# Compressed attention for eight heads at once, with block-diagonal keys and values, in a two-block transformer kernel

## The reference

```python
dist = (t[:, None] - cmp_end[None, :]).astype(jnp.float32)
valid = dist >= 0
s = jnp.einsum('bghqd,bgnd->bghqn', q_c, k_cmp) * scale
s = jnp.where(valid, s - slopes * dist, NEG)
p_cmp = jax.nn.softmax(s, axis=-1) * valid.any(-1, keepdims=True)
o_cmp = jnp.einsum('bghqn,bgnd->bghqd', p_cmp, v_cmp)
...
o = g_c[0] * o_cmp + g_c[1] * o_slc + g_c[2] * o_win
```

## Time and profile before

| what | value |
|---|---|
| median of 3 runs | 1159.49 us (1159.38 to 1160.04) |
| the profiled execution, its own time | 1160.29 us |
| its span, first to last instruction | 1158.5 us |
| PE busy | 1083.8 us, 94% |
| DVE busy | 666.1 us, 57% |
| ACT busy | 510.3 us, 44% |
| POOL busy | 64.1 us, 6% |
| attention, from the MLP of the compressed keys to `b_out` | 355.5 to 467.5 us |

### The profile page before, as it was taken

One profiled execution on the slowest core, in us unless ns is written; L12 is line 12 of the kernel. 1 busy time (PEld: TensorE's weight loads), 2 busy tenths in 40 slices (PEclk: granted clock), 3 DMA queues, 4 the chain that ended last, 5 costly groups with the idle time before them and its releaser, 6 DMA issues.

```text
span 1158.5 us, 17658 instructions
## 1 busy us (share of the span) xinstructions
PE 1083.8 (94%) x7447; PEld 959.1 (83%) x7447; DVE 666.1 (57%) x1099; ACT 510.3 (44%) x780; POOL 64.1 (6%) x103
## 2 busy tenths in 40 slices
PE   6985999999999977999999998999998989999997
PEld 6863799999989854799999987899666978999996
DVE  4975456555556498555555567646444535555554
ACT  5322344343443377454443444435344544444442
POOL 3000084000010000000000000000000000000000
PEclk9997999999997998999999999999899999999999
DMA  8765247666656300647666644553224505565540
GB/s 230 197 194 133 75 144 219 184 180 186 200 106 205 111 1 1 204 144 216 187 179 188 202 136 145 184 182 110 73 73 145 169 14 182 185 215 175 189 146 37
DMA packets 192633, 175.14 MB, mean 151 GB/s; under 512 B 15878, under 2 KB 168326, under 8 KB 192554
## 3 DMA queue, kind: packets, MB, share of 16 engines
q1 hardware_dynamic: 190584, 170.69, 48.6%
q10 hardware_dynamic: 1874, 3.30, 0.8%
q0 software_dynamic: 96, 0.02, 0.0%
HBM read 172.06 MB, written 1.93 MB: 150 GB/s over the span
## 4 chain that ended last, share of the span: by engine, by line
PE 82%; DVE 11%; ACT 3%; DMA 2%; issue 1%; SPq 1%; POOLq 0%; POOL 0%; ACTq 0%; DVEq 0%
PE bank L1630 24%; PE bank L1631 24%; PE bank L1632 24%; DVE split_lo L995 2%; PE bank L1798 2%; ACT split_hi L622 1%; DVE soft L1273 1%; DVE soft L1292 1%; PE bank L1655 1%; DMA act<-u_rows 1%; PE bank L1645 1%; DVE v L1367 1%; DVE xn_lo L1012 1%; PE bank L1866 1%; PE bank L2057 1%
## 5 line engine op out<-in xcount | busy, mean ns | idle before, releaser
L995 DVE TENSOR_TENSOR split_lo<-raw,split_hi 128x2048 fp32r<-128x2048 f32 (+1 forms) x157 | 355.7, 2271 | 195.3 <-ACT split_hi L622 195.2
L1630 PE MATMUL bank<-xn_hi,split_hi 128*128 128x256 f32 x1440 | 413.2, 287 | 5.7 <-DVE split_lo L995 3.5
L1631 PE MATMUL bank<-xn_lo,split_hi 128*128 128x256 f32 x1440 | 409.5, 284 | 0.0
L1632 PE MATMUL bank<-xn_hi,split_lo 128*128 128x256 f32 x1440 | 409.3, 284 | 0.0
L622 ACT ACTIVATE split_hi<-raw 128x2048 fp32r<-128x2048 f32 (+1 forms) x157 | 296.0, 1889 | 153.9 <-PE bank L1632 146.1
L1630 PEld LDWEIGHTS bank<-xn_hi,split_hi 128*128 128x128 f32 x1440 | 278.1, 193 | 12.2 <-issue 4.4
L1631 PEld LDWEIGHTS bank<-xn_lo,split_hi 128*128 128x128 f32 x1440 | 278.2, 193 | 1.4
L1632 PEld LDWEIGHTS bank<-xn_hi,split_lo 128*128 128x128 f32 x1440 | 278.0, 193 | 0.0
L1630 PE MATMUL bank<-split_hi,ffa_hi 128*128 128x512 f32 x320 | 125.4, 392 | 1.8 <-DVE ffa_lo L995 1.8
L1631 PE MATMUL bank<-split_lo,ffa_hi 128*128 128x512 f32 x320 | 125.0, 391 | 0.0
L1632 PE MATMUL bank<-split_hi,ffa_lo 128*128 128x512 f32 x320 | 124.6, 389 | 0.0
(11 more groups left out here) (281 smaller groups left out, 942.0 us busy)
## 6 DMA issues: line engine op xcount, KB each, us to landing
raw<-in_ffn_w_in SPq DMA_DIRECT2D x88, 512.0 KB, 5.1
raw<-in_w_ff SPq DMA_DIRECT2D x32, 1024.0 KB, 5.2
raw<-in_ffn_w_out SPq DMA_DIRECT2D x22, 1024.0 KB, 4.9
raw<-in_w_in SPq DMA_DIRECT2D x14, 1024.0 KB, 5.2
raw<-in_a_pw_w SPq DMA_DIRECT2D x16, 512.0 KB, 7.0
raw<-in_w_xkv SPq DMA_DIRECT2D x8, 1024.0 KB, 5.2
raw<-in_a_pw_w SPq DMA_DIRECT2D x4, 1024.0 KB, 5.8
raw<-in_b_w_in SPq DMA_DIRECT2D x4, 1024.0 KB, 6.1
```

What stands on the lines that cost most here:

```text
L995: return nc.vector.tensor_tensor(dst, src, hi.bitcast(F32), ALU.subtract)
L1630: mm(dst, left[0], right[0], start=start, stop=False)
L1631: mm(dst, left[0], right[1], start=False, stop=False)
L1632: return mm(dst, left[1], right[0], start=False, stop=stop)
```

## The change

The compressed branch leaves the loop over heads. For each group g its eight heads run together, in steps of their own.

- `kcmp` and `vcmp` go. ACT writes the compressed keys twice into `cmp_k`, block-diagonally: rows 0 to 63 (the even head of a pair) in columns 0 to 14 and rows 64 to 127 (the odd head) in columns 16 to 30, zeros elsewhere. So one matmul with all 128 rows of `qT` and 32 columns makes the scores of two heads. For the values ACT writes the hidden layer of the MLP four times for each head parity, spread over 128 columns (`cmp_hid`), so that the product with `phi2` comes out block-diagonal as well (`cmp_v`).
- POOL clears the place of these tensors once, in the first FFN stage.
- `cmp_scores(g)` on PE: four pairs times two t, eight matmuls of 32 columns into bank 6+g. Group 0 comes before chunk 3 of q, group 1 before the scores of heads 2 and 3.
- `cmp_shift(g)` on DVE: add the bias, maximum over each head's 16 columns, subtract it; three instructions over 256 elements a row, the first two each followed by a wait for itself (`link`). `cmp_exps(g)` on ACT is one exponential. `cmp_weigh(g)` on DVE: sum, reciprocal, product with the gate, product with the weights, the first three linked.
- The transposes of 15 columns go. For g = 0 in `nsa_turn(1)` and for g = 1 in `nsa_turn(5)` two transposes of 128 columns turn the weights of eight heads, and there DVE and ACT copy 128 columns more in `nsa_evac`.
- The two products with the values of a pair become one, with 32 rows, 128 output columns of weights and 256 moving columns.
- `NSA_PIECES` has four pieces instead of six.

```diff
+        CMP_TURN = [1, 5]
...
+            nc.gpsimd.memset(u[:, 5:8, PAD:PAD + S], 0.0).then_inc(cmp_zero, 1)
...
+            def cmp_exps(g):
+                sc.wait_ge(cmp_shifted, g + 1)
+                part = cmp_s[:, :, P * g:P * g + P]
+                nc.scalar.activation(part, part, ACT.Exp, scale=DH ** -0.5).then_inc(cmp_exp, 1)
...
-            nc.scalar.activation(hid[:, :, :].rearrange("p b n -> p (b n)"), bank[7][0:DH, 0:4 * NCMP],
-                                 ACT.Silu).then_inc(kv_act, 1)
+            nc.scalar.activation(hid[:, 0, :], bank[7][0:DH, 0:2 * NCMP], ACT.Silu)
+            sc.wait_ge(cmp_zero, 1)
+            for g in range(GROUPS):
+                for e in range(2):
+                    at = (2 + g) * NCMP
+                    x = nc.scalar.activation(cmp_hid[:, g, e, :, e, 0:NCMP], bank[7][0:DH, at:at + NCMP].unsqueeze(1)
+                                             .broadcast_to([DH, 4, NCMP]), ACT.Silu)
...
                 if b == 3:
                     nsa_exp(0)
+                    cmp_exps(0)
...
+                if i in CMP_TURN:
+                    nc.scalar.activation(cmp_t[:, CMP_TURN.index(i), P:S], bank[5][:, 384:512], ACT.Copy)
+                nc.scalar.activation(dst[:, 384:768], bank[5][:, 0:384], ACT.Copy).then_inc(pt_act, 1)
...
+            def cmp_shift(g):
+                ve.wait_ge(cmp_score, g + 1)
+                ve.wait_ge(bias_built, 8 * g + 8)
...
+                link(x)
+                top = cmp_stat[:, g, 0:16].rearrange("p (t h) -> p t h", t=TT)
+                link(nc.vector.tensor_reduce(top, s, AX.X, ALU.max))
+                nc.vector.tensor_tensor(s, s, top.unsqueeze(3).broadcast_to([P, TT, 8, 16]),
+                                        ALU.subtract).then_inc(cmp_shifted, 1)
+
+            def cmp_weigh(g):
+                ve.wait_ge(cmp_exp, g + 1)
...
+                link(nc.vector.tensor_reduce(total, s, AX.X, ALU.add))
+                link(nc.vector.reciprocal(share, total))
+                link(nc.vector.tensor_tensor(share, share, gate_of[:, :, 0, 8 * g:8 * g + 8], ALU.mult))
+                nc.vector.tensor_tensor(s, s, share.unsqueeze(3).broadcast_to([P, TT, 8, 16]),
+                                        ALU.mult).then_inc(cmp_weighed, 1)
             nsa_shift(0)
+            cmp_shift(0)
             q_scaled(3)
             nsa_shift(1)
             nsa_normed(0)
+            cmp_weigh(0)
             for p in range(HEADS // 2):
                 if 2 * p + 2 < HEADS:
                     nsa_shift(2 * p + 2)
+                if p == 0:
+                    cmp_shift(1)
                 nsa_evac(2 * p)
+                if p == 1:
+                    cmp_weigh(1)
                 nsa_normed(2 * p + 1)
...
-                for t in range(TT):
-                    for e in range(2):
-                        mm(bank[e][:, S + 16 * t:S + 16 * t + NCMP], qT[lanes[e], p, tok(t)], kcmp[lanes[e], g, :],
-                           start=True, stop=True)
...
+            def cmp_scores(g):
+                te.wait_ge(q_ready, 2 * g + 2)
+                for p in range(4 * g, 4 * g + 4):
+                    for t in range(TT):
+                        at = P * t + 32 * (p % 4)
+                        x = mm(bank[6 + g][:, at:at + 32], qT[:, p, tok(t)],
+                               cmp_k[:, g, :, :].rearrange("p e n -> p (e n)"), start=True, stop=True)
+                x.then_inc(cmp_score, 1)
...
+                        for e in range(2):
+                            at = S + P * g + DH * e
+                            x = mm(bank[7][:, at:at + DH], cmp_hid_g[:, g, e, :], phi2[:, 1, :],
+                                   start=True, stop=True)
...
-                for e in range(2):
-                    mm(dst[e], vcmp[:, d], w[e][0:NCMP, 768:1024], start=False, stop=True).then_inc(pv_done, 1)
+                j = slice(32 * (p % 4), 32 * (p % 4) + 32)
+                mm(bank[6 + p % 2][:, 0:S], cmp_v[j, g, :], cmp_t[j, g, :], start=False, stop=True).then_inc(pv_done, 2)
```

More of the change, by code:

```diff
@@ L262, in build_kernel @@
         window_ready = sem("window_ready")
+        cmp_zero = sem("cmp_zero")
+        cmp_score = sem("cmp_score")
+        cmp_shifted = sem("cmp_shifted")
+        cmp_exp = sem("cmp_exp")
+        cmp_weighed = sem("cmp_weighed")
         kv_dve = sem("kv_dve")
@@ L781, in _ @@
                     nsa_exp(0)
+                    cmp_exps(0)
                 if b == 0:
                     sc.wait_ge(phi_done, 3)
-                    nc.scalar.activation(kcmp[:, :, :].rearrange("p g n -> p (g n)"),
-                                         bank[7][:, 64:64 + GROUPS * NCMP], ACT.Copy)
-                    nc.scalar.activation(vcmp[:, :], bank[7][0:NCMP, P:2 * P], ACT.Copy).then_inc(kv_act, 1)
+                    for e in range(2):
+                        d = slice(DH * e, DH * e + DH)
+                        nc.scalar.activation(cmp_k[d, :, e, 0:NCMP], bank[7][d, 64:64 + GROUPS * NCMP]
+                                             .rearrange("p (g n) -> p g n", g=GROUPS), ACT.Copy)
+                    nc.scalar.activation(cmp_v[:, :, :], bank[7][:, S:2 * S].rearrange("p (g c) -> p g c", g=GROUPS),
+                                         ACT.Copy).then_inc(kv_act, 1)
             def nsa_evac(i):
@@ L809, in _ @@
                         out_hi(2 * p, xn[0][:, p - 1, :], bank[6 + (p - 1) % 2][:, 0:S])
+                    if i == 1:
+                        cmp_exps(1)
             out_hi(HEADS, xn[0][:, HEADS // 2 - 1, :], bank[7][:, 0:S])
@@ L1265, in nsa_shift @@
                 for n, piece in enumerate(NSA_PIECES):
[L1266 to L1269, removed]
+                    t, branch = n // 2, n % 2
+                    if t == 0:
                         src, bias = bank[i % 2][:, piece], biases[:, i, 0:P]
                     else:
-                        src, bias = bank[2 + i % 2][:, S * (branch - 1):S * branch], biases[:, i, P:3 * P]
+                        src, bias = bank[2 + i % 2][:, S * branch:S * branch + S], biases[:, i, P:3 * P]
                     x = nc.vector.tensor_tensor_reduce(out=scores_of(i)[:, piece], in0=src, in1=bias,
@@ L1311, in nsa_normed @@
                 nsa_weigh(i)
+            def cmp_shift(g):
+                ve.wait_ge(cmp_score, g + 1)
+                ve.wait_ge(bias_built, 8 * g + 8)
+                s = cmp_s[:, :, P * g:P * g + P].rearrange("p t (h n) -> p t h n", n=16)
+                x = nc.vector.tensor_tensor(s, bank[6 + g][:, 0:S].rearrange("p (t h n) -> p t h n", t=TT, n=16),
+                                            biases[:, 8 * g:8 * g + 8, 3 * P:3 * P + 32]
+                                            .rearrange("p h (t n) -> p t h n", t=TT), ALU.add)
+                link(x)
[5 more added lines that the diff above has]
+                ve.wait_ge(cmp_exp, g + 1)
+                s = cmp_s[:, :, P * g:P * g + P].rearrange("p t (h n) -> p t h n", n=16)
+                total = cmp_stat[:, g, 16:32].rearrange("p (t h) -> p t h", t=TT)
+                share = cmp_stat[:, 2 + g, 0:16].rearrange("p (t h) -> p t h", t=TT)
+                link(nc.vector.tensor_reduce(total, s, AX.X, ALU.add))
[3 more added lines that the diff above has]
+                                        ALU.mult).then_inc(cmp_weighed, 1)
             nsa_shift(0)
+            cmp_shift(0)
             q_scaled(3)
@@ L1896, in _ @@
                     nsa_score(0)
+                    cmp_scores(0)
                 if b == 2:
@@ L1908, in _ @@
                     for g in range(GROUPS):
-                        x = mm(bank[7][0:NCMP, P + DH * g:P + DH * g + DH],
-                               hid[:, 1, NCMP * g:NCMP * g + NCMP], phi2[:, 1, :], start=True, stop=True)
+                        for e in range(2):
+                            at = S + P * g + DH * e
+                            x = mm(bank[7][:, at:at + DH], cmp_hid_g[:, g, e, :], phi2[:, 1, :],
+                                   start=True, stop=True)
                     x.then_inc(phi_done, 1)
@@ L1920, in nsa_turn @@
                 turns = [(4, 0, 0), (4, P, 288), (4, 2 * P, 416), (5, 0, 128), (5, P, 544), (5, 2 * P, 672)]
+                if i in CMP_TURN:
+                    g = CMP_TURN.index(i)
+                    te.wait_ge(cmp_weighed, g + 1)
+                    for t in range(TT):
+                        nc.tensor.transpose(bank[4 + t][:, 384:512], cmp_s[:, t, P * g:P * g + P], ident[:, :])
                 for b, at, src in turns:
[L1922 to L1925, removed]
+                    x = nc.tensor.transpose(bank[b][:, at:at + P], s[:, src:src + P], ident[:, :])
                 x.then_inc(p_turned, 1)
@@ L1932, in nsa_pv @@
                     te.wait_ge(o_ready, p - 1)
+                else:
+                    te.wait_ge(cmp_shifted, p + 1)
                 g = p // (HEADS // GROUPS // 2)
@@ L1942, in nsa_pv @@
                            start=False, stop=False)
```

(6 more changed lines are left out.)

29 lines of the change are left out of this document (16 added, 13 removed).

## The result

The changed kernel takes 1152.94 us (median of 7 runs, 1151.32 to 1160.02), the kernel before 1159.49 in 7 runs beside it (1156.39 to 1161.83): a ratio of 0.9949, 95% interval 0.9927 to 0.9971. The forecast was 1154.8, ratio 0.9959.

The account below looks back on a forecast made before the run. DVE was taken to set the loop's pace, with PE's added work ahead of it bare. Terms: -9.4 (loop savings) + 3.6 (once on DVE) + 1.95 (PE ahead) - 0.9 (loop end) = -4.7 us, from 1159.5 to 1154.8; range 1151.8 to 1158.3.

Parts of the forecast that it names:

- Saving per head: DVE in the loop: small shifts, copies and multiplications go, 0.67 us a head, -9.4 us over 14.
- Start of the loop to the turn of head 14: DVE: -9.4 us saved, +1.26 `cmp_shift(1)`, +1.25 `cmp_weigh(1)`, +0.42 extra copy columns, +0.5 turn of head 1.
- the turn of head 1: First pair of the loop: PE at 1.2 GHz after a longer pause, less DVE work beside it, +0.5 us waiting.
- PE's margin: Between turns of an even and odd head: PE needs 2.65 us, DVE 2.89, so PE just fits, 0.2 to spare.
- Ahead of the loop on PE: Bare PE work before the loop: `cmp_scores(0)` +1.4 us net and value half of `phi` +0.55, together +1.95.
- The value half of `phi`: PE ahead of the loop: eight instructions instead of four, with 128 weight columns, +0.55 us (bounds 0.3 and 0.6).
- `cmp_weigh(0)`: DVE before the loop's first shift, where it had waited 0.53 us for scores: +0.14 us.
- End of the loop: PE from the turn of head 14 to `b_out`: four small transposes and a small copy go, -0.9 us.
- The first: Rival: second spell at the lower clock at the loop's start, costing 1.65 us or more, time 1156.9; chance 0.22.
- The second: Rival: low-clock spell at the loop's end vanishes, 2.4 us back, time 1152.4; chance 0.13.
- The third: Rival: lower clock stays through the loop, 4.1 us a pair more, 1163.0 with two pairs; chance 0.05.
- The fourth: Rival: PE binds the loop instead of DVE, so no effect, time 1159.3; chance 0.05.

Follow-up runs that it names:

- e3: Changed kernel without the compressed branch's scores, softmax, transposes and value products, MLP kept; 1146.27 us, ratio 0.9887 to the kernel before.
- e2: The changed kernel, unedited, timed and profiled once more; 1156.92 us, ratio 0.9972 to the kernel before.
- e1: The kernel before, unedited, profiled once more; 1158.39 us in one run.
- e8: Changed kernel with the first eight heads' scores behind chunk 3 of q and their shift on DVE later, uncovered; 1151.94 us in one run.
- e9: The changed kernel, unedited, run again on another chip; 1156.99 us, ratio 0.9951 to the kernel before.
- e10: Changed kernel with compressed weighing on POOL, group 1's scores behind those of heads 2 and 3, nine useless matmuls in PE's pauses; 1153.17 us, ratio 0.9910.
- e5: Changed kernel with `cmp_scores(0)` issued twice ahead of chunk 3 of q; 1158.36 us in one run.
- e6: Changed kernel with compressed weighing on POOL instead of DVE and `cmp_scores(1)` behind the scores of heads 2 and 3; 1157.11 us, ratio 0.9966.

## Why the prediction was right

- **What binds.** DVE, as said: the pair with the branch and without it takes the same 6.14 us (e3).
- **Saving per head.** 7.46 - 6.14 = 1.32 us a pair against 1.34, so -9.2 against -9.4 over seven pairs.
- **Start of the loop to the turn of head 14.** The forecast's terms add up to -9.4 + 1.26 + 1.25 + 0.42 + 0.5 = -5.97. It was 53.16 before (405.07 to 458.23) and 47.18 in e2 (404.09 to 451.27): -5.98. In the profiled execution it was 48.06, the 0.9 of the second low stretch above that. That the sum comes out to 0.01 is partly luck, for two terms missed in opposite directions. For p = 0 the forecast is -1.34 + 1.26 + 0.21 + 0.5 = +0.63, and the table has 8.54 (e2) against 8.22, +0.32. So the +0.5 for the turn of head 1 was about 0.2. For p = 2 the forecast is -1.34 + 0.21 = -1.13, and the table has 6.51 against 7.46, -0.95: the copy of head 5 cost 0.37 (6.51 - 6.14) instead of 0.21, and PE, now level with DVE, has two transposes more there. `cmp_weigh(1)` cost 1.29 (7.43 - 6.14) against 1.25.
- **PE's margin.** It was mis-sized. The prediction had PE ready in 2.65 us between the turns of an even and an odd head, with 0.2 to spare; PE takes 2.90 (431.50 to 434.40, without a wait). "I take 0.5" for the value product; it costs 0.65 (433.75 to 434.40), the upper bound. And the two small transposes gave back 0.23, not 0.32: the turn took 1.03 with them (420.90 to 421.93) and takes 0.80 without (431.50 to 432.30). The lost margin cost nothing measurable in the steady pairs.
- **Ahead of the loop on PE.** +1.95 forecast. At equal low time "to q" went from 43.6 (e1) to 45.6, and from 45.1 to 47.2 (e2): +2.0 and +2.1. `cmp_scores(0)` took 1.80 against 1.76. That 0.11 an instruction was so near is partly luck: the four of the earlier trace rows start at 348.65 and the next instruction at 349.02, 0.09 each, and their 0.46 in the chain includes the end of the last. The value half of `phi` was priced too low: +0.71 (1.03 - 0.32) against +0.55, above the bound of 0.6. By the page "TensorEngine Tiling (Array Packing)" of the Trainium skill, section Theoretical Speedup, I had worked out an estimate of 0.09 us an instruction; the rows give 1.80 / 16 = 0.11, so the measurement decides for the dearer price. In the first pair of profiles this term is hidden, 45.1 to 45.6, since the one before had 3.5 us more at the low clock.
- **`cmp_weigh(0)`.** First shift of the loop 4.64 us after the last matmul of q (397.21), before 4.46 (400.61): +0.18 against +0.14. `cmp_shift(0)` was free under its cover; in e8, without it, DVE was ready for that shift 5.98 us after q, 1.3 later, against the 1.26 said, and then waited 0.69 for the late scores.
- **End of the loop.** -0.9 forecast for the same low clock; this was mis-sized too. With 3.4 us at low clock in both it took 8.59 before (e1) and 8.06 after: -0.5. The -1.2 between the two first profiles and the -2.8 to e2 have in them that the one before had 6.8 us at the low clock there, the one after 3.4 and e2 none.
- **The rivals.** The first, a second low stretch at the start, came in the profiled execution and in e9, not in e2; but it also comes in the kernel before (e1). It cost 0.9 us, not 1.65, in a stretch where DVE and not PE sets the pace. The second, no low clock at the end, came in e2: 1.57 us back against the profile after, 2.4 predicted. With two profiles of one kernel and three of the other, whether the change makes either likelier isn't shown; within the changed kernel both come and go. The third did not occur: no steady pair was at the lower level. The fourth is refuted as put (no wait of DVE for PE in the steady pairs) though nearer than I thought.
- **The sum.** -4.7 us. Stretch by stretch at equal low time the changed kernel has +2.0 (to q), -5.8 (from q to the turn of head 14: 57.62 before, 51.83 in e2) and -0.5 (end of the loop), -4.3 in all. The stages as measured: -5.7 in the first two profiles, and with all executions of either kernel (112.0 and 112.6; 106.3, 105.5, 106.3) -6.3; of that up to 2.3 us is less time at the low clock (24.0 and 23.9 us against 20.5, 17.1 and 20.5, 4.6 less on average, and half of it where it is bare), so that the change itself gave 4.0 to 6.3. The medians give -6.5, -2.1 and -4.9 us on three occasions, and the forecast ratio of 0.9959 lies in all three intervals. The 6.5 of the first was partly luck.

What stays open: why the low stretches fall where they do in one execution and not in the next of the same kernel. PE's pauses are not enough to tell: e2 has 1.49 us ahead of the turn of head 3 and 2.36 ahead of that of head 14, as the profile after has (1.46, 2.36), and kept its clock behind both. And whether the POOL version beats the changed kernel: e10's median is lower, but the intervals overlap, and its profiled loop of 59.9 us isn't shorter than that of e2.

## What to carry to other kernels

Find the engine that sets the pace of a loop and count instructions on it: five small ones a head, none with much data, were worth 0.66 us of 3.7. Work taken out of a loop comes back once at its start, where pipelines are not yet filled and other engines idle; price that part by position, since here it gave back more than half of the gain. When a kernel's executions differ by more than the change is worth, compare stages of traces at equal clock before believing a difference of spans.

## What the hardware showed unexpectedly

- Behind 32 matmul instructions in a row, of 32 moving columns each, TensorE's granted clock fell from 2.4 to 1.2 GHz though its records show it busy throughout (e5 from 395.0, e8 from 399.9, granted clock 0.51 and 0.52). Nor is that new in the changed kernel: in the kernel before, the MLP's 128 instructions of 30 columns end at 363.07, others follow without a pause, and the clock falls at 364.1. Sixteen such instructions ahead of chunk 3, in every profile of the changed kernel, were not followed by a fall.
```profile
355.49 7.65 PE L1866 MATMUL bank<-pt,raw 128*64 128x30 f32 x128 [0.48 <-DVE pt L1224]
...
362.00:364.00 2.00, 2.00 (x29) 1.96 (x27) 1.94 (x4) 0.00 (x0) 0.00 (x0) 1.00 1.05 373
364.20:366.00 1.80, 1.80 (x10) 1.80 (x10) 1.14 (x2) 1.28 (x1) 0.00 (x0) 0.50 0.87 218
```
  The page "TensorE: Matmul & The Clock Gate" of the Trainium skill (Part 1) has activity release the throttle and idling bring it back; here a PE that its records show busy lost the clock, so busy time in a profile doesn't tell whether the clock holds.
- POOL's power of 16 elements a row took 2.92 us, where products of the same size take 0.22. In e6, timeline of POOL:
```profile
412.87 0.22 POOL L626 TENSOR_TENSOR cmp_stat<-u 128x16 f32<-128x16 f32 x1
413.17 2.92 POOL L628 TENSOR_TENSOR cmp_stat<-cmp_stat,nhalf 128x16 f32<-128x16 f32 x1
416.16 0.22 POOL L631 TENSOR_TENSOR cmp_stat<-gates,cmp_stat 128x16 f32<-128x16 f32 x1
```
- A product with 32 rows, 128 columns of weights and 256 moving columns took as long, 0.65 us, as the two of 15 rows and 64 columns that it replaces, which ran side by side.
